# Gate and up products of the feed-forward in two halves of 256 tokens, each half with its own weight loads

## What is computed

```python
h2 = rms_norm(x, norm2_w[layer]).astype(x.dtype)
hid = jax.nn.silu(h2 @ w_ffn_gate[layer]) * (h2 @ w_ffn_up[layer])
x = x + hid @ w_ffn_down[layer]
```

## Time and profile before

| | |
|---|---|
| time, median of 2 runs | 3485.1 us (3482.59 and 3487.61) |
| span of the profiled execution, first to last instruction | 3482.8 us |
| TensorE busy | 3405.5 us, 98%, 16463 matmuls |
| weight loads busy | 2795.0 us, 80%, 16463 loads |
| DVE, ACT, POOL busy | 1520.6, 1122.8 and 1690.2 us |
| mean granted TensorE clock | 0.991 |

### The profile page before, as it was taken

One profiled execution on the slowest core, in us unless ns is written; L12 is line 12 of the kernel. 1 busy time (PEld: TensorE's weight loads), 2 busy tenths in 40 slices (PEclk: granted clock), 3 DMA queues, 4 the chain that ended last, 5 costly groups with the idle time before them and its releaser, 6 DMA issues.

```text
span 3482.8 us, 42722 instructions
## 1 busy us (share of the span) xinstructions
PE 3405.5 (98%) x16463; PEld 2795.0 (80%) x16463; DVE 1520.6 (44%) x1852; ACT 1122.8 (32%) x1769; POOL 1690.2 (49%) x1413
## 2 busy tenths in 40 slices
PE   7999999999998999999899999999999999999999
PEld 6777787777677888888578888888888888888887
DVE  3655555555567888874432033311331133213320
ACT  4433324434234554553342232212221122112221
POOL 4533333333348888886365434443444444434443
PEclk9999999999999999999899999999999999999999
DMA  5444454343364555554544323323332333233323
GB/s 171 133 130 127 135 149 124 116 118 91 91 156 117 126 145 126 134 123 113 197 138 133 109 85 96 96 89 105 96 96 91 103 96 96 90 102 96 96 90 114
DMA packets 663947, 404.30 MB, mean 116 GB/s; under 512 B 191487, under 2 KB 595131, under 8 KB 663291
## 3 DMA queue, kind: packets, MB, share of 16 engines
q1 hardware_dynamic: 663802, 402.37, 40.1%
HBM read 347.05 MB, written 54.53 MB: 115 GB/s over the span
## 4 chain that ended last, share of the span: by engine, by line
PE 50%; DVE 1%; ACT 0%; POOL 0%; issue 0%; DVEq 0%; ACTq 0%; POOLq 0%
PE f_bank L149 9%; PE f_bank L151 9%; PE f_bank L150 9%; PE f_bank L2042 5%; PE f_bank L2043 5%; PE f_bank L2041 5%; PE f_bank L2000 2%; PE f_bank L2002 2%; PE f_bank L2001 2%; PE f_bank L1943 1%; PE f_bank L1944 1%; PE f_bank L1945 1%; PE f_bank L1952 0%; PE f_bank L1978 0%; POOL w_lo_b L140 0%; ACT w_hi_b L133 0%
## 5 line engine op out<-in xcount | busy, mean ns | idle before, releaser
L140 POOL TENSOR_TENSOR w_lo_b<-w_raw_b,w_hi_b 128x2048 fp32r<-128x2048 f32 (+1 forms) x152 | 681.9, 4486 | 929.3 <-ACT w_hi_b L133 929.3
L1285 POOL TENSOR_TENSOR ring_w_rounded<-ring_w_plain,ring_w_hi 128x1024 fp32r<-128x1024 f32 x138 | 334.0, 2422 | 594.2 <-ACT ring_w_hi L1298 594.2
L133 ACT CAST w_hi_b<-w_raw_b 128x2048 fp32r<-128x2048 f32 (+1 forms) x152 | 283.1, 1862 | 838.3 <-PE f_bank L2043 376.1
L149 PE MATMUL f_bank<-act_rounded,w_lo_b 128*128 128x512 f32 x1408 | 549.1, 390 | 2.3 <-POOL w_lo_b L140 1.2
L151 PE MATMUL f_bank<-act_rounded,w_hi_b 128*128 128x512 f32 x1408 | 547.8, 389 | 0.0
L150 PE MATMUL f_bank<-act_rounded,w_hi_b 128*128 128x512 f32 x1408 | 547.8, 389 | 0.0
L1597 PE MATMUL slab_ps<-h_hi,ring_w_rounded 128*128 128x512 f32 x1088 | 447.0, 411 | 2.8 <-DVE h_lo L1434 2.5
L1599 PE MATMUL slab_ps<-h_hi,ring_w_hi 128*128 128x512 f32 x1088 | 426.4, 392 | 0.0
L1598 PE MATMUL slab_ps<-h_lo,ring_w_hi 128*128 128x512 f32 x1088 | 426.1, 392 | 0.0
L149 PEld LDWEIGHTS f_bank<-act_rounded,w_lo_b 128*128 128x128 f32 x1408 | 264.3, 188 | 57.4 <-issue 2.3
L151 PEld LDWEIGHTS f_bank<-act_rounded,w_hi_b 128*128 128x128 f32 x1408 | 264.3, 188 | 54.9
(11 more groups left out here) (381 smaller groups left out, 5630.0 us busy)
## 6 DMA issues: line engine op xcount, KB each, us to landing
ring_w_plain<-in_w_in_dram SPq DMA_DIRECT2D x190, 512.0 KB, 4.1
w_raw_b<-in_w_ffn_gate_dram SPq DMA_DIRECT2D x44, 1024.0 KB, 5.1
w_raw_b<-in_w_ffn_up_dram SPq DMA_DIRECT2D x44, 1024.0 KB, 5.1
w_raw_b<-in_w_ffn_down_dram SPq DMA_DIRECT2D x32, 1024.0 KB, 5.0
zt<-slab_out SPq DMA_DIRECT2D x65, 256.0 KB, 4.3
w_raw_b<-in_w_out_dram SPq DMA_DIRECT2D x16, 1024.0 KB, 5.0
w_raw_b<-in_w_ffn_down_dram SPq DMA_DIRECT2D x16, 768.0 KB, 4.3
zt<-lout SPq DMA_DIRECT2D x40, 256.0 KB, 4.6
```

The source lines that it names most:

```text
L133: act.copy(g.w_hi[n.slot][:, 0:k, :], g.w_raw[n.slot][:, 0:k, :]).then_inc(g.w_hi_ready, 1)
L140: pool.tensor_tensor(g.w_lo[n.slot][:, 0:k, :], g.w_raw[n.slot][:, 0:k, :], g.w_hi[n.slot][:, 0:k, :].bitcast(F32), ALU.subtract).then_inc ...
L149: pe.matmul(bank, wl, hi[:, ka, :], start=start and j == 0, stop=False)
L1285: pool.tensor_tensor(raw_half(w_lo, h), raw_half(w_raw, h), hi_half(h).bitcast(F32), ALU.subtract).then_inc(lo_ready, 1)
```

## The change

In products each block's three matmuls over 512 tokens become six, three over tokens 0 to 255 and three over tokens 256 to 511, each into its half of the same bank. Every matmul is still issued with its own weight load, so the same weights are loaded once more for the second half. The accumulation is opened by the first matmul of the first half alone, and skip_group_check turns off a check of the builder on that. Nothing else is changed; later lines move down by 4 (L2067 becomes L2071).

```diff
 def products(pe, g, n, ks, bank, hi, lo, start=True, stop=True):
 
     ins = None
+    half = SEQ // 2
     for j, (kw, ka) in enumerate(ks):
         wh, wl = g.w_hi[n.slot][:, kw, :], g.w_lo[n.slot][:, kw, :]
-        pe.matmul(bank, wl, hi[:, ka, :], start=start and j == 0, stop=False)
-        pe.matmul(bank, wh, lo[:, ka, :], start=False, stop=False)
-        ins = pe.matmul(bank, wh, hi[:, ka, :], start=False, stop=stop and j == len(ks) - 1)
+        for at in (0, half):
+            o, h, l = bank[:, at:at + half], hi[:, ka, at:at + half], lo[:, ka, at:at + half]
+            first = start and j == 0 and at == 0
+            pe.matmul(o, wl, h, start=first, stop=False, skip_group_check=True)
+            pe.matmul(o, wh, l, start=False, stop=False, skip_group_check=True)
+            ins = pe.matmul(o, wh, h, start=False, stop=stop and j == len(ks) - 1, skip_group_check=True)
     return ins
```

## The result

The changed kernel takes 3537.2 us, median of 2 runs (3535.19 and 3539.26), against 3485.1 us before. The ratio is 1.0153, its 95% interval 1.0124 to 1.0183: 1.5% slower, and inside the 2% that I counted as "same". Forecast were 3541 us.

What follows compares the result with a forecast made beforehand. TensorE was taken to bound the kernel, alone in the feed-forward. A fixed 13.3 ns on each of 4224 split matmuls, all else at nothing, gave 3485.1 + 56.3 = 3541.4 us, range 3480 to 3600.

Steps and rivals of the forecast that it cites:

- The sum: Gate and up products: each of 4224 matmuls becomes two of 120.0 ns instead of 226.7, +56 us, 3541 us.
- Fixed or by the column: Whether the 13.3 ns over a 512-column stream are paid per matmul (taken, 0.42) or grow with the columns (0.30).
- The rival by the column: Feed-forward products: the extra goes with the columns, 113.3 ns a half, 0 to +11 us, 3485 to 3496 us; chance 0.30.
- First, the extra is not the load's.: Matmuls with unhidden loads show about the same drain for both kinds, so the 13.3 ns belong to the stream.
- Second, plain matmuls show almost none.: Plain 4-byte matmuls, streamed at half rate, take only 2 or 3 ns over their stream, at 256 and 512 columns.
- One that takes data as fast as it comes can't [fetch ahead], and then pays the change each time.: Full-rate streams pay 13.3 ns at each change of instruction, whatever their length; half-rate streams can hide it.
- The load comes out of its cover: In a half, load and stream hinder each other: 128.5 ns a half, +128 us, 3613 us; chance 0.20.
- The load is the bound: The load sets the pace and the extra vanishes: 111.7 ns a half, 3471 us; chance 0.04.
- The feed of instructions, and the jump: Instructions limited to 136 ns each, +192 us, 3677 us, or the loop's jump uncovered, up to 172 us; chance 0.04.
- What costs nothing: POOL, ACT, DVE and the loop's jump in the feed-forward stay covered behind TensorE's longer slabs, costed at 0.

Runs made afterwards that it cites:

- e4: Changed kernel with only the up slabs in halves, gate slabs whole: 3507.1 us, ratio 1.0063.
- e10: Kernel before with every gate and up matmul at 384 moving columns, later tokens left out: 3271.9 us, against 3476.7 beside it.
- e5: Kernel before with halves as in the change, but 64 instead of 128 stationary columns in 15 of 16 blocks: 3485.5 us, ratio 1.0012.
- e9: Kernel before with stationary columns read 1, 2 or 4 elements apart, gate slabs at 512 moving columns, up slabs at 256: 3392.6 us.
- e8: Kernel before with loads 128, 96, 64 and 32 columns wide, gate slabs at 512 moving columns, up slabs at 256: 3442.4 us.
- e7: Kernel before with constant 2-byte (bf16) operands in 15 of 16 blocks, 512 columns in blocks 1 to 7, 256 in 8 to 15: 3251.6 us.
- e11: Kernel before with 512 moving and 64 stationary columns in every gate and up matmul: 3488.5 us, against 3476.7 beside it.
- e2: Changed kernel with four quarters of 128 columns in place of two halves, each matmul with its own load: 4409.1 us, ratio 1.2654.
- e12: Kernel before with 192 moving columns and a 128-wide load in every gate and up matmul, each issued twice: 3462.7 us.
- e1: Kernel before with 512, 384, 256 and 128 moving columns within each gate or up slab, four blocks each: 3240.4 us.
- e6: Changed kernel with tokens cut 384 + 128 instead of 256 + 256: 3733.1 us, ratio 1.0725.

## Why the prediction was right, and where its reason was not

- **The sum.** Forecast 120.0 ns a half, 4224 x 13.3 = +56.3 us and 3541 us; measured 120.0 ns, +55.5 us in the last part, 3537.2 us by the median. The median rose by 52.1 us; the 3.4 us between are within what the earlier phases do from one execution to the next (the last part began at 2033.1 us before, at 2032.3 after and at 2027.7 in e4).
- **Fixed or by the column.** Right, and now at three lengths: 226.7, 173.3 (e10) and 120.0 ns are 213.3, 160 and 106.7 plus 13.3 each. The rival by the column, with 0.30, needed 113.3 and 170 ns. 113.3 appeared only with another load and output (e5).
- **"First, the extra is not the load's."** This step failed. It was drawn from rows where no load ran beside the matmul and allowed 10 ns of error against a price of 13.3. e9 changed nothing but how the load is read, and 512 columns went from 226.7 to 233.3 ns and more; e5 halved load and output, and 6.7 of the 13.3 ns went. I should have seen that rows which agree within 10 ns can't decide about 13.
- **"Second, plain matmuls show almost none."** This was read more finely than the rows allow: 1.02 - 0.592 has an error of 5 ns or so. At 512 columns the step is 433 ns (see e8), 7 over its stream and not 2 or 3, half of the 13.3.
- **"One that takes data as fast as it comes can't [fetch ahead], and then pays the change each time."** Half right. The whole 13.3 ns were seen only with 4-byte values at full rate: 2.4 are left with 2-byte values (e7), none at half the clock (e8), some 7 for plain values. But it isn't paid for the change of instruction alone, or e9 would have kept 226.7. What fits the runs is that a load and a 4-byte stream at full rate get in each other's way. That this is a collision, and in what, is argued, not shown. Nor is it the whole price: at 256 columns 6.7 ns stayed with 64 and with 32 stationary columns alike (e5, e8), so half may be the stream's own. Why half a load costs less beside 256 columns and more beside 512 (e5, e11) stays open. The direct test, a rounded matmul with no load beside it, is in no run.
- **How much was luck.** Each matmul has one load, so a fixed price per load and one per matmul give the same +56 us, and the wrong owner did no harm to the sum. But the choice of fixed over by the column, 0.42 against 0.30, rested on two arguments, of which the first failed and the second was a misread row. That it came out right is in part luck.
- **The load comes out of its cover** (0.20). Its price didn't come: loads took 192 instead of 188 ns and the steps stayed at 120.0. Its mechanism, a load and a stream in each other's way, is nearer to what e9 shows than my own. **The load is the bound** (0.04) points at a real floor, 112 ns (e2, e12), and the halves lie 8 ns above it. I read that floor rightly from the earlier trace rows.
- **The feed of instructions, and the jump** (0.04). Out for this change: e2 holds 112 ns for 898 pairs, and the jump shows no gap. In e10, with 384 columns, two steps at each change of group are long.
- **What costs nothing.** Right: from 2033 us on POOL's wait for ACT grew from 829 to 883 us, and TensorE still waited once for POOL, 0.8 us where it was 1.2.

## What to carry to other kernels

In a chain of rounded 4-byte matmuls, each with a fresh and contiguous 128 x 128 load, one costs the larger of 112 ns and its columns at 2.4 GHz plus 13.3 ns, as measured at 512, 384, 256, 192 and 128 columns. So cutting the moving side costs 13 ns a piece down to 256 columns. Below some 236 columns, an estimate from 111.7 - 13.3 = 98.4 ns of stream, the load takes over and each further piece costs its full 112 ns (1.5% here for halves, 27% for quarters). Keep 512 columns, and if pieces must be, make them equal. To find a price per instruction, measure at three lengths without changes of shape in between, and vary load, stream and output one at a time before naming whose it is.

## What I had not expected of the hardware

- Changing the load alone moves the pace of the stream: at 512 columns 226.7 ns with a contiguous load and 233.3 with one of stride 2 (e9). With load and output narrower, 256 columns go from 120.0 ns to 113.3 (64 or 32 stationary columns, e5, e8) and 512 columns from 226.7 to 230.0 (64, e11). The Trainium skill (page TensorE: Matmul & The Clock Gate, section Step-by-step: what each phase is for, under LDWEIGHTS) says that loading the next weights doesn't take read bandwidth from the running matmul. For 2-byte values the trace agrees, as far as 2.4 ns over the stream can show it (e7). For 4-byte ones the pace does depend on how the load reads; whether it is read bandwidth that they share no run here shows.
- After a change of shape or a pause the pace takes some six steps to settle (e1: 177 ns on average, then 173.3; e10 at the start of some slabs), and 64-wide loads at 512 columns never settle (224 to 236 ns, e11).
- At 1.2 GHz the price is gone: 427 ns for 512 columns (e8), while the granted clock was 0.50.
- A load doesn't run ahead by more than one matmul: behind a 384-column matmul the load of the second 128-column one starts only with the first (2200.45 and 2200.44 in e6).
- Loads with a stride of four elements bound the pace at 233 ns, about twice the 112 of contiguous ones (e9).
